# A transformer kernel on one core: stick-breaking attention with the keys on the partitions

## The reference, cut to what matters

```
lost[q,k] = softplus(z[q,k]) = max(z, 0) + log(1 + exp(-|z|))      for k < q, else 0
w[q,k]    = exp(z[q,k] - sum over j >= k, j < q of lost[q,j])      for k < q, else 0
out[q]    = sum over k of w[q,k] * v[k]
```

## Time and profile before

| | us |
|---|---|
| median of 3 runs (lowest, highest) | 5031.83 (5019.65, 5035.23) |
| the profiled execution's own time | 5035.78 |
| its span, first to last instruction | 5034.0 |
| TensorE busy in it | 4482.8 (89%) |
| TensorE, mean granted clock (1 is 2.4 GHz) | 0.941 |

### The profile page before, as it was taken

One profiled execution on the slowest core, in us unless ns is written; L12 is line 12 of the kernel. 1 busy time (PEld: TensorE's weight loads), 2 busy tenths in 40 slices (PEclk: granted clock), 3 DMA queues, 4 the chain that ended last, 5 costly groups with the idle time before them and its releaser, 6 DMA issues.

```text
span 5034.0 us, 90473 instructions
## 1 busy us (share of the span) xinstructions
PE 4482.8 (89%) x38676; PEld 3131.1 (62%) x38676; DVE 2228.4 (44%) x3897; ACT 1502.9 (30%) x2632; POOL 791.7 (16%) x499
## 2 busy tenths in 40 slices
PE   6899899988998899979998988878999988878999
PEld 3566666666555554464443965656787955656787
DVE  2555555453355542130112457446434357446343
ACT  2343333332222211010001334443332234443232
POOL 0021111110232230000000321233000321233000
PEclk9899999988999999989999999989999998989999
DMA  6100000000111024238998211114221211114221
GB/s 231 64 33 16 8 19 17 5 26 13 42 46 38 34 90 183 99 121 357 407 409 355 91 61 41 66 52 160 101 96 76 81 61 41 69 53 155 101 101 51
DMA packets 86825, 512.06 MB, mean 102 GB/s; under 512 B 10504, under 2 KB 11032, under 8 KB 45848
## 3 DMA queue, kind: packets, MB, share of 16 engines
q1 hardware_dynamic: 86424, 506.28, 26.3%
HBM read 476.85 MB, written 29.38 MB: 101 GB/s over the span
## 4 chain that ended last, share of the span: by engine, by line
PE 71%; DVE 13%; issue 7%; ACT 3%; DMA 3%; PEld 1%; POOL 1%; SPq 0%; PEldq 0%; DVEq 0%; POOLq 0%; ACTq 0%
PE ps L229 68%; PE ps L232 3%; DVE upper L248 2%; DVE upper L240 2%; ACT upper L287 2%; DMA upper<-in_ew 2%; DVE lower L240 2%; DVE upper L264 2%; PEld ps L229 1%; DVE upper L244 1%; DVE upper L256 1%; DVE rounded L240 1%; ACT lower L287 1%; DVE upper L260 0%; POOL upper L3702 0%
## 5 line engine op out<-in xcount | busy, mean ns | idle before, releaser
L229 PE MATMUL ps<-rounded,rounded 128*128 128x512 f32 (+2 forms) x7968 | 1672.4, 369 | 45.9 <-POOL rounded L3237 21.6
L229 PEld LDWEIGHTS ps<-rounded,rounded 128*128 128x128 f32 x7968 | 1345.9, 194 | 307.5 <-issue 36.0
L229 PE MATMUL ps<-lower 128*128 128x512 f32 (+10 forms) x4976 | 1078.0, 393 | 55.4 <-issue 22.8
L229 PE MATMUL ps<-upper 64*64 64x64 f32 (+8 forms) x15584 | 840.6, 260 | 173.0 <-DVE upper L264 38.9
L287 ACT ACTIVATE upper<-ps 128x512 f32<-128x512 f32 (+6 forms) x953 | 440.2, 491 | 1649.7 <-PE ps L229 1229.0
L229 PEld LDWEIGHTS ps<-upper 64*64 64x64 f32 (+4 forms) x15584 | 598.7, 145 | 445.7 <-issue 185.5
L229 PEld LDWEIGHTS ps<-lower 128*128 128x128 f32 (+3 forms) x4976 | 578.1, 184 | 442.9 <-issue 376.9
L229 PE MATMUL ps<-lower,upper 64*64 64x64 f32 (+6 forms) x7248 | 607.8, 304 | 52.1 <-DMA lower<-in_ada 21.3
L2616 POOL TENSOR_TENSOR rounded<-lower,rounded 128x1024 fp32r<-128x1024 f32 (+2 forms) x90 | 273.0, 3035 | 2009.3 <-ACT rounded L287 2009.0
L287 ACT ACTIVATE upper<-upper 128x512 f32<-128x512 f32 (+9 forms) x693 | 342.7, 501 | 648.7 <-DVE upper L260 167.9
L229 PEld LDWEIGHTS ps<-lower,upper 64*64 64x64 f32 (+3 forms) x7248 | 335.0, 143 | 263.1 <-issue 195.1
(11 more groups left out here) (89 smaller groups left out, 2444.5 us busy)
## 6 DMA issues: line engine op xcount, KB each, us to landing
lower<-in_ew SPq DMA_DIRECT2D x140, 1024.0 KB, 10.4
upper<-in_ew SPq DMA_DIRECT2D x52, 1024.0 KB, 12.9
lower<-in_b0f SPq DMA_DIRECT2D x16, 2048.0 KB, 7.5
lower<-in_b1f SPq DMA_DIRECT2D x16, 2048.0 KB, 7.8
upper<-in_ada SPq DMA_DIRECT2D x18, 1024.0 KB, 5.2
lower<-in_wrkv SPq DMA_DIRECT2D x8, 1728.0 KB, 7.1
lower<-in_b0g SPq DMA_DIRECT2D x24, 512.0 KB, 3.8
gad<-upper SPq DMA_DIRECT2D x48, 256.0 KB, 3.7
```

Of the source, the lines that this page charges most:

```text
L229: return self.e.matmul(out, lhsT, rhs, start=start, stop=stop)
```

## The change

The unit becomes a whole head, with the keys on the partitions and the queries along the free axis. For the key block j only the queries from 128 j on matter, so the four blocks have 512, 384, 256 and 128 columns, together 1280, and lie in three PSUM banks; two heads are under way at a time. The mask for the diagonal blocks is added on TensorE, by a product of the identity and a table (-1e30 where the key is not before the query). ScalarE takes Abs from PSUM, copies the scores to SBUF, and does Exp and Ln; VectorE makes lost = max(z, 0) + log(...), rounds it and takes the rest, so that two fp32r halves stand for it. TensorE then adds, into the same PSUM banks, minus the sums over later keys, as products of the halves with a triangle of -1 for the block itself and a square of -1 for later blocks (20 matmuls). VectorE adds the result to the copied scores, ScalarE takes the exp, and this is already laid out as TensorE needs it for the values, so nothing is transposed. GpSimd has no part in it. The scale 1/8 moves into the copies of the unit c0 (the queries). The planner has two generators, one for even and one for odd heads, with 1.78 filler items behind each round.

```diff
@@ block2_map
-    b.trip = [RA[:, 1536 * z:1536 * z + 1536] for z in range(6)]
+    b.soft = [k.plain(at + 3840 * z, 1280) for z in range(2)]
+    b.chance = [k.plain(47272 + 1280 * z, 1280) for z in range(2)]
+    b.lost = [k.rounded(at + 3840 * z + 1280, 1280) for z in range(2)]
+    b.raw = [k.plain(at + 3840 * z + 2560, 1280) for z in range(2)]
+    b.rest = [k.rounded(at + 3840 * z + 2560, 1280) for z in range(2)]
+    b.sums = k.rounded(at + 7680, 256)
...
@@ block2_order
+    def heads(z):
+        for _ in range(3 * z):
+            yield None
+        for hh in range(z, 8, 2):
+            for s in (0, None, None, 1, None, 2):
+                yield None if s is None else ("stick", hh, s)
...
-    drain([lane("stick", 32, 5, z) for z in range(6)], filler, 1.4)
+    drain([heads(z) for z in range(2)], filler, 1.78)
...
+BLOCK_AT = (0, 512, 1024, 896)
+def block_cut(j, i=None):
+    at = BLOCK_AT[j] + 128 * ((i or j) - j)
+    return slice(at, BLOCK_AT[j] + 512 - 128 * j)
...
@@ block2_tensor
+    def stick(hh, s):
+        team, slot, use = k.lane[hh % 2], hh % 2, ("stick", l, hh)
+        e = slice(64 * slot, 64 * slot + 64)
+        if s == 0:
+            ps = banks.take_at(use, 3 * slot, 3)
+            for j in (0, 1, 3, 2):
+                pe.mm(ps[:, block_cut(j)], b.ck[e, hh // 2, 128 * j:128 * j + 128], b.cq[e, hh // 2, 128 * j:512], j != 3, False)
+                last = pe.mm(ps[:, BLOCK_AT[j]:BLOCK_AT[j] + 128], pe.ident, k.c2["sb"], False, j != 1)
+            last.then_inc(team.pe.up("score", l, hh), 1)
+            return
+        ps = k.pair(use)
+        if s == 1:
+            pe.wait_ge(M.act, "sums", l)
+            pe.wait_ge(team.dve, "parts", l, hh)
+            pe.wait_ge(team.act, "kept", l, hh)
+            for j in (3, 2, 1, 0):
+                for i in range(j, 4):
+                    for part in (b.lost[slot], b.rest[slot]):
+                        last = pe.mm(ps[:, block_cut(j, i)], b.sums[:, 128:256] if i > j else b.sums[:, 0:128],
+                                     part[:, block_cut(i)], ...)
+            last.then_inc(team.pe.up("less", l, hh), 1)
+        else:
+            pe.wait_ge(team.act, "exp", l, hh)
+            for i in range(4):
+                for j in range(i + 1):
+                    p = b.chance[slot][:, BLOCK_AT[j] + 128 * (i - j):BLOCK_AT[j] + 128 * (i - j) + 128]
+                    for half in (slice(0, 64), slice(64, 128)):
+                        last = pe.mm(ps[half, 1280 + 64 * i:1344 + 64 * i], p[:, half], b.cv[:, j, 64 * hh:64 * hh + 64],
+                                     j == 0, j == i)
+            last.then_inc(team.pe.up("value", l, hh), 1)
+            banks.give(use, team.dve, "value", l, hh)
...
@@ block2_vector
+            if t == "c0":
+                v.ts(P.dve, dst, ps, 0.125, MUL, event=use)
...
+    def stick(hh, s):
+        team, slot = k.lane[hh % 2], hh % 2
+        t, ps = team.dve, k.pair(("stick", l, hh))
+        if s == 0:
+            v.wait_ge(team.act, "log", l, hh)
+            v.stt(t, b.raw[slot], ps[:, 0:1280], 0.0, b.soft[slot], MAX, ADD)
+            v.copy(t, b.lost[slot], b.raw[slot])
+            v.tt(t, b.rest[slot], b.raw[slot], b.lost[slot].bitcast(F32), SUB, "parts", l, hh)
+        elif s == 1:
+            v.wait_ge(team.pe, "less", l, hh)
+            v.tt(t, b.chance[slot], b.chance[slot], ps[:, 0:1280], ADD, "less", l, hh)
+        else:
+            v.wait_ge(team.pe, "value", l, hh)
+            v.copy(t, b.otC[:, :, 64 * hh:64 * hh + 64], v3(ps[:, 1280:1536], 64), "value", l, hh)
...
@@ block2_scalar
+    def stick(hh, s):
+        team, slot = k.lane[hh % 2], hh % 2
+        t, ps, p = team.act, k.pair(("stick", l, hh)), b.soft[slot]
+        if s == 0:
+            if hh == 0:
+                a.copy(M.act, b.sums[:, 0:128], c2["tri"])
+                a.copy(M.act, b.sums[:, 128:256], c2["one"], "sums", l)
+            a.wait_ge(team.pe, "score", l, hh)
+            a.act(t, p, ps[:, 0:1280], AF.Abs)
+            a.copy(t, b.chance[slot], ps[:, 0:1280], "kept", l, hh)
+            a.act(t, p, p, AF.Exp, scale=-1.0)
+            a.act(t, p, p, AF.Ln, "log", l, hh, bias=1.0)
+        elif s == 1:
+            a.wait_ge(team.dve, "less", l, hh)
+            a.act(t, b.chance[slot], b.chance[slot], AF.Exp, "exp", l, hh)
...
@@ block2_gpsimd
-            if s == 2:
-                y, r = o.buf[:, 0:o.nk], o.buf[:, 1024:1024 + o.nk]
-                g.wait_ge(o.lane.dve, "sum", *o.u)
-                g.wait_ge(o.lane.pool)
-                g.e.tensor_tensor(y, y, r, SUB).then_inc(o.lane.pool.up("less", *o.u), 1)
```

More of the change, by code:

```diff
@@ L70, in consts @@
     q, k = i[:, None], np.arange(512)[None] - 384
-    p2 = {"mla": add(k <= q), "sb": add(k < q), "g2": add((k <= q) & ((q - k) % 4 == 0)),
+    p2 = {"mla": add(k <= q), "sb": add(i[:, None] < i[None]), "tri": -f(i[:, None] >= i[None]), "one": -f(up | True), "g2": add((k <= q) & ((q - k) % 4 == 0)),
           "g3": add((k <= q) & ((q - k) % 16 == 0))}
@@ L307, in take, with take_at @@
         self.i = i + n if i + n < self.hi else self.lo
+        for b in range(i, i + n):
+            assert self.free.get(b, ()) is not None, "no bank is free"
+            if self.free.get(b):
+                self.pe.wait_ge(*self.free[b])
+            self.free[b] = None
+        self.pe.k.bank[use] = (i, n)
+        return self.pe.k.ps[:, 512 * i:512 * (i + n)]
+    def take_at(self, use, i, n):
         for b in range(i, i + n):
@@ L3027, in attend @@
         o = Unit(k, l, name, u)
-        L, stick = o.lane, name == "stick"
+        L = o.lane
         if s == 0:
@@ L3033, in attend @@
             banks.give(use, L.dve, "score", *o.u)
-        elif s == (3 if stick else 2):
+        elif s == 2:
             use = ("turn", *o.u)
@@ L3040, in attend @@
             last.then_inc(L.pe.up(*use), 1)
-            banks.give(use, L.dve if stick and o.i % 2 else L.act, *use)
-        elif s == (4 if stick else 3):
+            banks.give(use, L.act, *use)
+        elif s == 3:
             use = ("value", *o.u)
             ps = banks.take(use)
-            pe.wait_ge(L.dve if stick and o.i % 2 else L.act, "turn", *o.u)
+            pe.wait_ge(L.act, "turn", *o.u)
             n = o.nk // 128
@@ L3051, in attend @@
             banks.give(use, L.dve, *use)
+    def stick(hh, s):
[17 more added lines that the diff above has]
+                        last = pe.mm(ps[:, block_cut(j, i)], b.sums[:, 128:256] if i > j else b.sums[:, 0:128],
+                                     part[:, block_cut(i)], j != 1 and i == j and part is b.lost[slot],
+                                     j != 3 and i == 3 and part is b.rest[slot])
+            last.then_inc(team.pe.up("less", l, hh), 1)
[9 more added lines that the diff above has]
+            banks.give(use, team.dve, "value", l, hh)
     for name, *z in b.order:
@@ L3057, in block2_tensor @@
             rope(*z)
-        elif name in ("softA", "softB", "stick"):
+        elif name in ("softA", "softB"):
             attend(name, *z)
+        elif name == "stick":
+            stick(*z)
         elif name == "lat_turn":
@@ L3269, in dense @@
                 v.wait_ge(k.stored[slot_of(t, i)[0]], "gad", l, *slot_of(t, i)[1])
[L3270 removed]
+            if t == "c0":
+                v.ts(P.dve, dst, ps, 0.125, MUL, event=use)
+            else:
+                v.copy(P.dve, dst, v3(ps, 256)[:, :, 0:tok_width(t)] if name == "tok" else ps, *use)
     def soft(name, u, s):
@@ L3493, in block2_scalar @@
 def block2_scalar(k, a, l):
-    b, M, P, tail = k.b2[l], k.main, k.proj, k.tail
+    b, M, P, tail, c2 = k.b2[l], k.main, k.proj, k.tail, k.c2
     def dense(name, t, i, s, dst):
@@ L3504, in dense @@
                 a.wait_ge(k.stored[slot_of(t, i)[0]], "gad", l, *slot_of(t, i)[1])
-            a.copy(P.act, dst, v3(ps, 256)[:, :, 0:tok_width(t)] if name == "tok" else ps, *use)
+            a.act(P.act, dst, v3(ps, 256)[:, :, 0:tok_width(t)] if name == "tok" else ps, AF.Copy, *use, scale=0.125 if t == "c0" else 1.0)
     def soft(name, u, s):
```

18 lines of the change are left out of this document (1 added, 17 removed).

## The result

The changed kernel takes **5120.04 us** (median of 4 runs, 5113.22 to 5124.87), the kernel before 5033.53 in the runs beside it: ratio 1.0177, 95% interval 1.0154 to 1.0199. The forecast was 5079 with a range up to 5109: the sign and the place were right, the size was not. I expected 47 us more, there are 86.

A forecast was written before the change was run, and what follows sets the result against it. No engine is full; the latency of one unit's chain bounds stage C. Per layer 165.7 + 10 collisions + 7 clock = 182.7 us, 23.5 above 159.2; two layers add 47 to 5031.8, giving 5079, range 5036 to 5109.

The forecast's parts named there:

- The place and the bound: Only stage C of each layer changes, 159.2 us before; no engine is full, one unit's chain ends TensorE's waits.
- The order: Stage C: head B's values wait for all of head A's chain, at 16.2 us; loop 37.0 us for two heads.
- The durations on ScalarE and VectorE: Stage C, per head: ScalarE 5.0 us for four passes, last exp 1.3; VectorE's first phase 3.9, copy 0.95 in it.
- TensorE's pieces: Stage C, per head at full clock: scores 3.9 us, triangle sums 2.8, values 1.4, together 8.1.
- Scores: Stage C, TensorE per head: products 2.7 us, masks 0.95, changes of kind 0.25, together 3.9.
- GpSimd beside VectorE: Stage C: five GpSimd splits a layer hold up VectorE's copy and subtraction 2 us each, 10 in all; bounds 0 and 12.5.
- Clock: Stage C: TensorE runs at 1.2 GHz behind gaps, 1.3 us lost at each; 5 to 9 per layer, 7 taken.
- rival C: Stage C: low clock through most chain pieces, collisions at bound, copy at 1.5; 198 us per layer, 5109 total; chance 0.15.
- The base: Stage C, walked through in issue order at full clock with nothing in the way: 165.7 us per layer, 6.5 more than before.

## Why the prediction was right in sign and wrong in size

- **The place and the bound.** Right: only stage C changed, by the same amount in both layers, and the chain through ScalarE and VectorE ends TensorE's waits. The kernel before was limited that way too, and the change put larger pieces on the chain.
- **The order.** Right: B's values wait behind A's four passes and A's first phase, 3296.97 - 3277.13 = 19.8 us after A's scores; 16.2 by my sum, and with the scores' measured 7.7 instead of 3.9 that is 20.0. Eleven gate steps are bare at the end (66 products, 15.45 us).
- **The durations on ScalarE and VectorE.** Right within a few per cent: two passes from PSUM 2.51 us, two in SBUF 2.58, softplus sum and subtraction 1.49, the value copy 0.42. For the copy I chose 0.95 between 0.95 and 2.8; it is 0.83. The Trainium skill, "VectorE: DVE Perf Modes", section "The perf-mode tier table", gave an estimated 0.8, and the trace agrees.
- **TensorE's pieces.** Values 1.31 us from start to start (1.4), sums 2.92 (2.8): right. **Scores** 4.40 instead of 3.9: wrong by 0.5 for each of 8 heads, **4 us per layer**. The step that failed is "for the changes that the pairs' times don't hold yet I add 0.25": alternating costs 1.17 us more than grouping. The rest of the term erred the other way: products and masks without changes stood at 2.7 + 0.95 = 3.65, and grouped they take 3.23.
- **GpSimd beside VectorE.** Right: 10.4 us per layer against 10, and in the first head and four more, as counted; 3.6 of them in the first head, where two splits ran and the subtraction met one too, and 1.7 in each other, where I had 2 for each. The Trainium skill, "SBUF — State Buffer", section "SBUF: two separate sides", calls it a lock held for the whole instruction; the copy of 0.83 that takes 2.4 to 2.5 beside a split of 2.4, and 0.83 in all eight heads once the splits are held, agrees.
- **Clock.** This step failed, and it is the main error: a fixed loss for each gap. I had four gaps of 5 us at 1.3 each, "and the three before A's scores, lengthened by the splits to 4, may do it too": 7. It measured **16.2 us per layer**. The 1.3 came from one gate step behind a gap, and I carried the same 1.3 to every gap. But what is lost grows with the work that is done before the clock rises again: the scores of a third, fifth and seventh head lose 3.3 us each (7.7 against 4.4), 10 together, the first sums 1.7, values up to 1.0 (2.40 against 1.39), and the steps behind them the rest. Scores, sums and values all stand on the chain. My rival C, "the low clock stays through most of the chain pieces", was the case that came, and it allowed twice the 7; but it reached 198 per layer only with a copy 4.4 dearer than mine and collisions 2.5 dearer, and had nothing for the scores.
- **The base.** Right within some 3 us: 199.6 less 16.2 (clock), 10.4 (collisions) and 4.0 (scores) leaves 169.0, against 165.7. I can't assign these 3 us; the experiments show that the terms aren't independent (holding the splits took 16 us, not 10.4, as shorter gaps gave back clock).
- **Outside the stage.** 3.4 us of the span and the scatter of the medians; none of it was in the sum.

So of the 40.6 us of a layer, the base's 6.5, the collisions' 10.4, the clock's 16.2 and the scores' 4.0 make 37.1. The forecast lacked 17 us in each layer; the two terms that were mis-sized, clock (9.2 too little) and scores (4.0), hold 13 of them.

## What to carry to other kernels

When a change lets larger pieces of TensorE's work stand behind a wait, price the clock by the pieces: all that stands behind the gap on the chain, at its length at the low clock (here 7.7 instead of 4.4 us), and not a fixed sum for each gap. Two matmul shapes that use different numbers of rows are issued in blocks, not in turn. And a method is not judged by the first order in which it is issued: the same products were 1.8% slower than the old kernel in one order, and 0.5% faster than it, as it stood, in another, in which sums go first, GpSimd's splits stay out of VectorE's SBUF passes and the filler reaches to the end.

## What the runs showed of the hardware that I had not expected

- Extra products that nobody reads made the kernel 33 us faster (5120.04 to 5087.35), with a granted clock of 0.96 instead of 0.82 in the part with the heads.
- Equal gaps had unequal results: sums behind waits of 2.40 to 2.44 us took 2.99, 3.83 or 4.55 us, and scores behind a wait of 2.42 began at full clock and lost it inside, without a further gap (6.08 us instead of 4.40). Two layers with the same instructions ended at 174.2 and 182.9 us.
- Alternating products of 64 and of 128 rows cost 1.17 us in 4.40 for eight products; in blocks they took 3.23.
- Making GpSimd, the engine with the least to do, wait took 16 us per layer off the stage.
